# A relative-position bias table built on 128 partitions and stored from the scalar engine's queue, in a two-layer hybrid streaming encoder on one core

## What is computed

```python
def half_ffn(x, norms, w_gu, w_down):
    h = rms_norm(x, norms[0])
    g, u = jnp.split(h @ w_gu, 2, axis=-1)
    return x + 0.5 * rms_norm((jax.nn.silu(g) * u) @ w_down, norms[1])

# in the attention of a block of queries:
bias = rel_bias[t5_bucket(idx - q_pos[None, :, None])].astype(jnp.float32)
s = jnp.einsum('bqhgd,bqjhd->bqhgj', q, k_sel) * (HEAD_DIM ** -0.5) + bias

# once for all layers:
p_lb = jax.nn.softmax(hgrn_lb_logits, axis=0)
lb_all = jnp.cumsum(p_lb, axis=0); lb_all = lb_all - lb_all[0]
```

## Time and profile before

| What | Value |
|---|---|
| runs | 3252.95, 3255.93, 3255.27 us |
| median | 3255.27 us |
| the profiled execution, first to last instruction (span) | 3254.3 us |
| its distance to the median | 1.0 us |
| TensorE matmul busy | 2851.5 us, 88% of the span |
| VectorE busy | 1528.1 us, 47% |
| ScalarE busy | 944.0 us, 29% |
| GpSimd busy | 476.2 us, 15% |
| moved by DMA | 209.51 MB, 64 GB/s on average |

### The profile page before, as it was taken

The page is one execution under the profiler, slowest core; times in us unless marked ns, Lnnn a source line. Parts: engine busy times, 40 slices in busy tenths (PEclk is TensorE's granted clock), DMA queues, the critical chain, the costliest instruction groups (busy, mean ns, idle before and its releaser), DMA issues. The chain is left out here.

```text
span 3254.3 us, 44093 instructions
## 1 busy us (share of the span) xinstructions
PE 2851.5 (88%) x18054; PEld 2665.5 (82%) x18054; DVE 1528.1 (47%) x1886; ACT 944.0 (29%) x1237; POOL 476.2 (15%) x328
## 2 busy tenths in 40 slices
PE   1999998997477979999969999989955788999997
PEld 1899998894354879999969999979834458999997
DVE  1633333528965353333353333352499644433333
ACT  1322223216423332212232212231362342322221
POOL 1100001105812120000120000020084313000001
PEclk9999999998768989999989999999976798999998
DMA  5122212113010212122112122122120111212211
GB/s 108 65 71 71 78 63 79 65 52 98 1 73 7 72 52 78 59 83 73 57 60 84 62 81 77 57 73 78 36 76 15 59 46 46 78 68 75 78 61 63
DMA packets 50676, 209.51 MB, mean 64 GB/s; under 512 B 13928, under 2 KB 14312, under 8 KB 34568
## 3 DMA queue, kind: packets, MB, share of 16 engines
q1 hardware_dynamic: 50568, 208.05, 19.3%
HBM read 197.85 MB, written 10.19 MB: 64 GB/s over the span
## 5 line engine op out<-in xcount | busy, mean ns | idle before, releaser
L291 PE MATMUL ps<-hr,wr 128*128 128x320 f32 x11424 | 1707.5, 311 | 83.6 <-DVE hr L407 65.7
L291 PEld LDWEIGHTS ps<-hr,wr 128*128 128x128 f32 x11424 | 1692.3, 189 | 99.7 <-DVE hr L407 43.5
L291 PE MATMUL ps<-hid,wr 128*128 128x320 f32 x4224 | 620.8, 309 | 0.0
L291 PEld LDWEIGHTS ps<-hid,wr 128*128 128x128 f32 x4224 | 619.8, 188 | 0.0
L286 DVE TENSOR_TENSOR wr<-stage,wr 128x2048 fp32r<-128x2048 f32 x184 | 421.7, 2292 | 299.7 <-ACT wr L282 299.7
L282 ACT ACTIVATE wr<-stage 128x2048 fp32r<-128x2048 f32 x184 | 350.6, 1905 | 557.5 <-PE ps L291 288.9
L548 DVE TENSOR_TENSOR arena<-ps,arena 128x640 f32<-128x640 f32 x88 | 72.5, 824 | 545.5 <-PE ps L291 543.8
L523 POOL TENSOR_TENSOR arena<-arena 128x640 f32<-128x640 f32 x28 | 44.3, 1582 | 1737.0 <-ACT arena L499 1737.0
L490 ACT ACTIVATE arena<-arena 128x640 f32<-128x640 f32 x88 | 65.1, 739 | 801.8 <-DVE arena L548 801.8
L860 POOL TENSOR_TENSOR proj<-proj,arena 128x640 f32<-128x640 f32 x120 | 200.1, 1669 | 33.6 <-ACT arena L1018 16.9
L938 PE MATMUL ps<-proj 128*128 128x256 f32 x264 | 90.9, 519 | 97.5 <-issue 78.4
(11 more groups left out here) (204 smaller groups left out, 2224.5 us busy)
## 6 DMA issues: line engine op xcount, KB each, us to landing
stage<-in_wgu SPq DMA_DIRECT2D x88, 1024.0 KB, 4.8
stage<-in_wd SPq DMA_DIRECT2D x32, 768.0 KB, 4.2
stage<-in_w_in SPq DMA_DIRECT2D x24, 1024.0 KB, 4.8
stage<-in_wd SPq DMA_DIRECT2D x32, 640.0 KB, 3.8
stage<-in_w_out SPq DMA_DIRECT2D x8, 1024.0 KB, 5.0
arena<-in_ic SPq DMA_DIRECT2D x16, 256.0 KB, 2.8
hf<-bias_table SPq DMA_DIRECT2D x2, 2048.0 KB, 10.7
arena<-in_kc SPq DMA_DIRECT2D x16, 256.0 KB, 5.2
```

Of the source, the lines that this page charges most:

```text
L291: mm = pe.matmul(out, w(s), v(t), start=start and n == 0, stop=stop and n == 2)
```

## The change

The table is computed with each head's column of `rel_bias` repeated over 128 columns of the stationary operand, so that every head's half row comes out on all 128 partitions at once. That takes 16 matmul calls (8 heads, 2 halves) in place of 2, over eight PSUM banks. The scalar engine takes the first half of each head out of PSUM, the vector engine the second half, after its softmax. The scalar engine's exponential comes ahead of its copies. The scalar engine, not SP, then issues the store, from 128 partitions of 8 rows each, to the same 8 x 128 x 656 tensor. SP no longer waits in the setup block, and its loads are reordered: `rel_bias`, `bucket_hot`, `lb`, `consts`, then `x`.

```diff
-        const_in, table_ready, table_out, ones_ready = (
-            sem(n, True) for n in ("const_in", "table_ready", "table_out", "ones_ready"))
+        const_in, table_act, table_out, ones_ready = (
+            sem(n, True) for n in ("const_in", "table_act", "table_out", "ones_ready"))
...
-        t_neg = scratch[0:8, 1024:1024 + NREL]
+        t_bias = scratch[:, 10112:10112 + 8 * NREL].rearrange("p (h n) -> p h n", h=8)
+        HREL = NREL // 2
+        LB_STEPS = 11
...
             @block.sync
             def _(sp):
-                for dst, src in ((cst[:], ins["consts"]), (t_rel, ins["rel_bias"]),
-                                 (t_hot, ins["bucket_hot"]), (t_lbe[:, 0:4], ins["lb"])):
+                for dst, src in ((t_rel, ins["rel_bias"]), (t_hot, ins["bucket_hot"]), (t_lbe[:, 0:4], ins["lb"]),
+                                 (cst[:], ins["consts"])):
                     sp.dma_start(dst, src).then_inc(const_in, 16)
                 sp.dma_start(x[:], ins["x"]).then_inc(x_in, 16)
-
-                sp.wait_ge(table_ready, 2)
-                sp.dma_start(ins["table"], t_neg.unsqueeze(1).to_broadcast([8, 128, NREL])).then_inc(table_out, 16)
...
                 pe.wait_ge(const_in, 64)
-                for c in range(2):
-                    pe.matmul(ps[0:8, c, 0:NREL // 2], t_rel, t_hot[:, c * (NREL // 2):(c + 1) * (NREL // 2)],
-                              start=True, stop=True).then_inc(table_mm, 1)
+                for n in range(16):
+                    hd, c = n // 2, n % 2
+                    if n >= 8:
+                        pe.wait_ge(*((table_act, hd - 3) if c == 0 else (lb_step, LB_STEPS + hd - 3)))
+                    pe.matmul(ps[:, n % 8, 0:HREL], t_rel[:, hd:hd + 1].to_broadcast([32, 128]),
+                              t_hot[:, c * HREL:(c + 1) * HREL], start=True, stop=True).then_inc(table_mm, 1)
...
             def _(act):
-
-                for c in range(2):
-                    act.wait_ge(table_mm, c + 1)
-                    act.activation(t_neg[:, c * (NREL // 2):(c + 1) * (NREL // 2)], ps[0:8, c, 0:NREL // 2],
-                                   ACT.Copy, scale=8.0).then_inc(table_ready, 1)
                 act.wait_ge(lb_step, 3)
                 act.activation(t_lbe[:, 0:4], t_lbe[:, 4:8], ACT.Exp).then_inc(lb_exp, 1)
+                for hd in range(8):
+                    act.wait_ge(table_mm, 2 * hd + 1)
+                    act.activation(t_bias[:, hd, 0:HREL], ps[:, 2 * hd % 8, 0:HREL], ACT.Copy,
+                                   scale=8.0).then_inc(table_act, 1)
+                act.wait_ge(table_act, 8)
+                act.wait_ge(lb_step, LB_STEPS + 8)
+                act.dma_start(ins["table"].rearrange("h p n -> p h n"), t_bias).then_inc(table_out, 16)
...
                 dve.tensor_scalar(lb_all[:, :, 2:4], lb_all[:, :, 0:2], -1.0, 1.0, ALU.mult, ALU.add).then_inc(lb_step, 1)
+                for hd in range(8):
+                    dve.wait_ge(table_mm, 2 * hd + 2)
+                    dve.tensor_scalar(t_bias[:, hd, HREL:], ps[:, (2 * hd + 1) % 8, 0:HREL], 8.0, None,
+                                      ALU.mult).then_inc(lb_step, 1)
```

## The result

The changed kernel takes 3224.16 us (median of four runs, 3222.43 to 3225.53) against 3255.60 us before (four runs, 3252.95 to 3257.67): a ratio of 0.9901, with a 95% interval of 0.9887 to 0.9915. That is 31.4 us less. The forecast was 3217.5 us with a range of 3211 to 3227. The direction and the place were right; the middle was 6.7 us too low. Nearest came the rival in which TensorE stays at its lower level, 3223.7 us, which had been given 0.13.

The account below looks back on a forecast made before the run. The opening was bound by weights waiting behind the 51 GB/s table store on SP's queue. Release at 28.2 for 65.99 us saves 37.8 of the 3254.3 span: 3216.5, plus 1.0 to the median, 3217.5 us; range 3211 to 3227.

Parts of the forecast that it names:

- the rival in which TensorE stays at its lower level: Table's matmuls: all 32 records at the lower clock, 17.4 us for 11.2, giving 3223.7 us; chance 0.13.
- The stage and the binding wait: Opening: the scalar engine's wait for the first weight tile binds; its release at 65.99 us moves everything behind one for one.
- The case that was given 0.76: Whole kernel: the main forecast, 3217.5 us, with the scalar engine released at 28.2 us.
- Loads: Setup: consts fourth land about 0.4 us later than `lb` did, so the table's matmuls start at 4.6 us.
- Matmuls: Setup: 32 records in 11.2 us, the clock rising after 4.9 us; end at 15.8; bounds 8.8 and 17.4.
- Copies, issue and barrier: End of setup: last copy to 16.3 us, store's issue 0.88 to 17.2, parameters issued at 18.2 after the barrier.
- Weights: Opening: release 7.77 us after the parameters' issue, plus 2.2 for overlap with the store, at 28.2.
- Sum to median: Whole kernel: 37.8 us off the 3254.3 span gives 3216.5; the median 1.0 above, 3217.5.
- The store's landing: Table store: landing at about 25 us costs nothing, its next waiter coming at about 72; up to 45 us slower still covered.
- The sentences on two queues: Store's queue: queues share 16 DMA engines, another saves issue time only, so 2.2 us overlap counts; otherwise 3215.3.
- The rival "store slow, weights pass it": Opening: replicated store no faster, weights pass it at 113 GB/s; release 35.7, time 3225.0 us; chance 0.07.
- The slower case: Opening: store keeps 51 GB/s and holds up weights from the other queue too; release 75.3, 3264.6 us; chance 0.02.

Follow-up runs that it names:

- the repeat: The changed kernel contracting over 128 rows, rows 32 to 127 filled with zeros, run again with no edit, five rounds: 3219.36 us, ratio 0.9884.
- the first run with zero rows: The changed kernel with its 16 matmuls contracting over 128 rows, rows 32 to 127 zeros: 3226.56 us (two runs), ratio 0.9902.
- the run with the queue alone: The kernel before, its 8-partition, two-matmul table stored from the scalar engine's queue in place of SP's: 3220.61 us against 3256.64, ratio 0.9893.

## Why the prediction was right, and where it was off

**The stage and the binding wait: right.** The opening was the only stretch that changed, and line 316 (324 after) stood 37.39 us behind the release in both kernels. The release moved by 31.4 us and so did the median. That these agree to a tenth is in part luck: the profiled span fell by 33.9 (3254.3 to 3220.4), because 3148.4 us remained behind the norm's sum for 3150.9 before, which is within the spread between executions.

**The range: right by its width.** The case that was given 0.76 did not happen. What happened at the matmuls was the rival given 0.13, and the range had been drawn to take in that rival.

**Loads: right.** Matmuls began at 4.67 for 4.6.

**Matmuls: the step that failed.** "I take that: 9 records in 4.9 us, the other 23 at 0.27" gave 11.2 us (its parts add up to 11.3); measured 17.85, the lower bound's pace throughout (17.4). The burst taken as a model had 128 contracted rows, the table has 32, and with 128 rows the same records take 10.76 and 11.05 us. The forecast compared the two kinds of matmul by columns alone. This term is 6.6 us, the whole miss of 6.4 in the release. One reading under it was loose too: 7 records of 256 columns in 2.00 us are 1.1 ns a column, not the 1.6 that the forecast read there. A window counts a record that lies across its edge in both windows: the changed kernel shows five records in 2.00 us, where its pace of 17.85 / 32 = 0.56 us, or 1.7 ns a column, makes 3.6.

**Copies, issue and barrier: right, and 0.7 us too dear.** From the last matmul to the parameters' issue 1.7 us passed for 2.4. The scalar engine's issue took 0.39 us, near the lower bound, and from its end to the parameters 0.70 passed for 1.0; the last copy took 0.50 for 0.45.

**Weights: right.** 10.35 us from issue to release, for 7.77 + 2.2 = 9.97. The overlap was priced at 2.2 and cost 2.6.

**Sum to median.** The forecast set the median 1.0 us above the span. In the profiled execution the device time is 2.0 us above the span (3222.43 for 3220.4), and the median of the runs is 1.7 above that. So the miss of 6.7 in the median is 6.4 from the release, less the 2.5 by which this execution ran shorter behind the norm's sum, and 2.8 more between span and median.

**The store's landing: covered, as said.** It landed 13.0 us after its issue, at 36.2 and not at about 25, behind the first weight tile; its waiter came at 78.56.

**The sentences on two queues: half right.** The rule that queues run on the same engines and that another one saves issue time only, from the Trainium skill, DMA: Bandwidth & Descriptors, Issuing engines are not separate DMA queues, holds here for a store at full rate: 34.59 against 34.88, and 20.59 against 21.39. For the slow store its second half does not hold: there the other queue brought the release from 65.99 to 32.70, which is 33.3 us, while the parameters' issue became shorter by 20.1 (20.44 to 0.35), and the measurement decides. The rival "store slow, weights pass it" had that mechanism with a release of 35.7 for the changed kernel's later build; with the old build it came at 32.70, 23.72 us behind the parameters' issue where the rival had 17.5. Bandwidth left over (113 GB/s) was too kind a price for passing a slow store.

**The slower case** needed both halves to fail. Each half works alone, so it was rightly small.

## What to carry to other kernels

A store on the queue ahead of loads costs what it takes to drain, so look at the rate at which it runs: 51 GB/s from 8 neighbouring partitions, about 205 from 8 partitions four apart, about 400 from 128. Two cures for one stall do not add: try each alone before paying for both, here 15.3 us of building for nothing over a queue that was free. When a short matmul burst stands on the path, price its rows as well as its columns, and prefer fewer matmuls: two that fill 128 output partitions gave the table that sixteen gave, and a kernel faster than both that were compared (3213.27 and 3210.08 us).

## What the runs showed that was not expected

- Back-to-back float32 matmuls over 32 rows kept a pace of about 0.55 us a record for 17.85 us; over 128 rows, 96 of them zeros, the same records sped up on the way and took 11.05 us, 11.77 in the repeat. The clock column reads 1.00 through both bursts and is no reading so early in this program. Behind the bursts the two kernels differ. These are windows of TensorE in the first run with zero rows, then one of the changed kernel:

```profile
18.00:20.00 2.00, 0.00 (x0) 0.76 1.02 399
28.00:40.00 12.00, 3.14 (x13) 0.50 0.41 164
```
```profile
28.00:40.00 12.00, 4.43 (x20) 1.00 0.73 274
```

  With zero rows the granted clock falls from 1.00 to 0.50 between 18 and 20 us, after a burst that ended at 15.84, so it had stood at the upper level (2.4 GHz). The changed kernel shows no such fall. Its 1.00 there is no reading either: its small matmuls of the squares (line 344) follow each other every 0.43 us, as those of the zero rows (line 346) do at 0.50.
- A transfer of 58.5 KB issued behind a store at 51 GB/s lands after 54.5 us on the same queue and after 19.2 us on another. Passing is possible, but not free: alone it takes 3.2 us in the median of all its issues in the kernel before.
- Behind the opening, where the programs are the same, profiled executions differ by up to 11.5 us (3147.1 us behind the norm's sum in the run with the queue alone, 3158.6 in the first with the zero rows). It goes with the mean granted clock of the whole execution: 3147.1 to 3151.1 us where that is 0.936 or 0.937, 3153.3 at 0.935, 3156.4 and 3156.7 at 0.934 and 0.933; and in the three over 128 rows, whose mean has an early stretch at 0.50 in it, 3150.6 at 0.931, 3155.1 at 0.930 and 3158.6 at 0.929. Why the clock differs between executions was not tried.
